# A layer's branches with finer points, twelve gate groups of the first merge made earlier, and a reordered start

## The reference

```
xn = RMSNorm(x);  z = xn @ w_in              # queries, keys, values, pool input, gates ...
ya = sliding-window attention (128) with sinks and a relative-position bias
yb = trailing means of windows 2/4/8/16 minus the token, @ w_pool
yc = mLSTM, chunks of 128, running-max stabiliser, gated and normed
merged = sum over a, b, c of sigmoid(g_b) * (y_b @ w_br_b)    # g_b: 1024 columns of z each
x = x + merged @ w_out
q = RMSNorm(x) @ wq;  top 16 x top 16 keys for 8 heads -> 16 experts a head, 128 a token
x = x + sum over 128 experts of gate * gelu(x . u[e]) * v[e]
```

## Time and profile before

| | us |
|---|---|
| median of three runs | 3836.78 |
| the execution profiled | 3825.35 |
| its span, first to last instruction | 3823.5 |
| TensorE busy | 3160.3 (83%) |
| VectorE busy | 2255.4 (59%) |
| ScalarE busy | 1102.1 (29%) |
| GpSimd busy | 1172.0 (31%) |
| read from and written to HBM | 344 GB/s over the span |
| mean granted clock of TensorE | 0.931 of 2.4 GHz |

### The profile page before, as it was taken

The page is one execution under the profiler, slowest core; times in us unless marked ns, Lnnn a source line. Parts: engine busy times, 40 slices in busy tenths (PEclk is TensorE's granted clock), DMA queues, the critical chain, the costliest instruction groups (busy, mean ns, idle before and its releaser), DMA issues. The chain is left out here.

```text
span 3823.5 us, 31573 instructions
## 1 busy us (share of the span) xinstructions
PE 3160.3 (83%) x10006; PEld 1820.0 (48%) x10006; DVE 2255.4 (59%) x5201; ACT 1102.1 (29%) x3314; POOL 1172.0 (31%) x1038
## 2 busy tenths in 40 slices
PE   7798879979989799769979799762699898777777
PEld 4487634546655444436656444431366563222222
DVE  1411777774657767664657688661555487775444
ACT  1210233432223324332223323340221233332222
POOL 0000333333333243333324233230233234443443
PEclk9899989989999899889999899885899999999999
DMA  5134899879999999779999899873899799999998
GB/s 168 60 124 159 348 365 383 349 297 396 420 394 403 365 403 412 303 303 404 420 384 407 349 403 398 324 266 139 331 375 392 278 399 397 421 421 422 421 420 358
DMA packets 204913, 1317.39 MB, mean 345 GB/s; under 512 B 23235, under 2 KB 27387, under 8 KB 72098
## 3 DMA queue, kind: packets, MB, share of 16 engines
q0 software_dynamic: 148608, 1082.20, 69.9%
q1 hardware_dynamic: 52681, 220.59, 15.4%
q10 hardware_dynamic: 3456, 12.58, 0.8%
HBM read 1298.97 MB, written 17.64 MB: 344 GB/s over the span
## 5 line engine op out<-in xcount | busy, mean ns | idle before, releaser
L1857 POOL DMA_INDIRECT arena<-uv,eidx x1032 | 1171.4, 1135 | 2623.2 <-PE ps L889 1889.5
L889 PE MATMUL ps<-arena,dgs 128*128 128x512 f32 x3412 | 1631.1, 622 | 268.4 <-ACT dgs L1189 244.4
L1428 DVE CUSTOM_DVE_ANT_0 arena<-arena,xx 128x1024 f32<-128x1024 f32 x1024 | 1231.8, 1220 | 583.9 <-DMA arena<-uv,eidx 559.5
L889 PEld LDWEIGHTS ps<-arena,dgs 128*128 128x128 f32 x3412 | 652.3, 198 | 1083.1 <-issue 675.0
L1170 ACT ACTIVATE gel<-dots 128x2 f32<-128x2 f32 x516 | 104.4, 202 | 1585.3 <-DVE dots L1428 1584.4
L922 PE MATMUL ps<-wbuf,xT 128*128 128x420 f32 (+1 forms) x1152 | 428.5, 522 | 7.7 <-DMA wbuf<-w_z 6.6
L1069 PE MATMUL ps<-xT,wbuf 128*128 128x256 f32 (+1 forms) x1536 | 356.8, 386 | 5.2 <-DMA wbuf<-w_merge 3.0
L1069 PEld LDWEIGHTS ps<-xT,wbuf 128*128 128x128 f32 x1536 | 295.1, 193 | 74.2 <-issue 19.4
L922 PEld LDWEIGHTS ps<-wbuf,xT 128*128 128x128 f32 (+1 forms) x1152 | 205.2, 181 | 231.1 <-issue 221.7
L1189 ACT ACTIVATE dgs<-cst,wgt 128x128 f32<-128x128 f32 x853 | 305.3, 395 | 16.7
L1662 DVE SCALAR_TENSOR_TENSOR T<-T,ps 128x256 f32<-128x256 f32 (+1 forms) x96 | 40.6, 423 | 434.5 <-PE ps L1073 434.5
(11 more groups left out here) (352 smaller groups left out, 1901.5 us busy)
## 6 DMA issues: line engine op xcount, KB each, us to landing
wbuf<-w_merge SPq DMA_DIRECT2D x96, 768.0 KB, 8.4
wbuf<-w_z SPq DMA_DIRECT2D x64, 840.0 KB, 8.6
wbuf<-w_q SPq DMA_DIRECT2D x64, 512.0 KB, 8.1
arena<-uv,eidx POOLq DMA_INDIRECT x1032, 11.4
wbuf<-w_o SPq DMA_DIRECT2D x32, 512.0 KB, 7.4
xin<-x_prompt SPq DMA_DIRECT2D x8, 1024.0 KB, 8.3
grow<-gains SPq DMA_DIRECT2D x8, 512.0 KB, 9.1
xin<-biasfull SPq DMA_DIRECT2D x4, 1024.0 KB, 4.9
```

What stands on the lines that cost most here:

```text
L889: done = mm(ps[:, half, :], dgs[:, j, :], ring[:, j, row_], start=(q == 0), stop=(q == P - 1), skip_group_check=True)
L1428: v.tensor_tensor_reduce(ring[:, j, 0:D], ring[:, j, 0:D], x, 1.0, 0.0, ALU.mult, ALU.add, dots[:, j:j + 1]).then_inc(s["dotted"], 1)
L1857: g.indirect_dma_start(ring[:, j, :], None, uv, bass.IndirectOffsetOnAxis(ap=experts, axis=0)).then_inc(got[j], 16)
```

## The change

- *Finer points.* `BRANCH` has 10 points of equal weight instead of 7; a stretch keeps its number of slots. Pass 1: 2, 2, 2, 2, 2, 0, 2, 2, 2, 2 slots a tile instead of 4, 2, 2, 2, 2, 2, 4; tile 0 of pass 2: 2, 2, 4, 2, 2, 2, 2, 2, 2, 4 instead of 4, 4, 2, 2, 4, 2, 6. The new TensorE places are behind S, behind the first scores (ahead of the 8-column broadcast), behind the inter-chunk product, behind the second scores, and on so to the end; ScalarE has its points 0 to 2 behind its three copies.
- *Order in a tile.* The cumulative sum (4 columns) is made first, into bank 3; the pool's means go to bank 7; VectorE copies the mLSTM's q behind the diagonal instead of ahead of it, and the second half of P ahead of the h chain.
- *Early gates.* In pass 0 the gates of the first 12 merge units are made in the branches, 6 a tile (1, 2, 1, 1, 1 behind points 2, 4, 6, 8, 9), into banks 0 and 1; ScalarE copies each to `early`, in the idle gather ring, and makes the tanh from there in the merge. Their weights come in two parts: the gates' two thirds behind the projection's weights, the branch third in the merge.
- *Start.* The tables but `cst` are issued behind the first two weights, the bucket matmul stands behind the projection's unit 0, `spread_bias` behind it as before, and the norm doesn't wait for them.
- *Tile by tile.* The projection's first unit waits for the xT of its tile only.

```diff
-BRANCH = (4, 4, 2, 2, 4, 2, 6)
+BRANCH = (2.4,) * 10
+EARLY = 12
+EARLY_AT = {2: 1, 4: 2, 6: 1, 8: 1, 9: 1}
...
             sp.dma_start(xin[:, :, :], x_prompt[0:NT].rearrange("t p d -> p t d")).then_inc(s["x_in"], 16)
-            sp.dma_start(cst[:, :], consts[:, 0:C_KEEP]).then_inc(s["setup"], 16)
...
+            sp.dma_start(cst[:, :], consts[:, 0:C_KEEP]).then_inc(s["consts_in"], 16)
+            def load_tables():
+                sp.wait_ge(s["init_v"], 1)
+                sp.dma_start(T[0:32, 512:520], rel).then_inc(s["setup"], 16)
+                sp.dma_start(T[:, 0:512], consts[:, C_KEEP:C_ALL]).then_inc(s["setup"], 16)
...
-                weights(w_z, ..., [lambda: load_bias(p)] if p else [spread_bias], ...)
+                weights(w_z, ..., [lambda: load_bias(p)] if p else [load_tables, spread_bias], ...)
+                if p == 0:
+                    weights(w_merge, (12, P), EARLY, s["gate_mm"], 0, 1, part=lambda i: (0, 2 / 3))
...
                 weights(w_merge, (12, P), 3 * KC, s["br_mm"], 3 * KC * p, 1, ...,
+                        part=lambda i: (2 / 3 if p == 0 and i < EARLY else 0, 1))
...
             def project(p):
...
                     for i, (t, rows_) in enumerate(tiles):
+                        if c == 0:
+                            pe.wait_ge(s["xT_ready"], norms(p, 0, i + 1))
...
+                    if p == c == 0:
+                        buckets()
+            def gates_early(units):
+                for u in range(gates_done[0], gates_done[0] + units):
+                    pe.wait_ge(w_in[u % 2], 16 * ((NZ + u) // 2 + 1))
+                    if u >= 2:
+                        pe.wait_ge(s["early_out"], u - 1)
+                    wv = wbuf[:, u % 2, 0:KC * P].rearrange("p (c n) -> p c n", c=KC)
+                    for c in range(KC):
+                        last = mm(ps[:, u % 2, 0:TOK], wv[:, c, :], xT[:, c, 0:TOK], start=(c == 0), stop=(c == KC - 1))
+                    last.then_inc(s["gate_mm"], 1)
...
                     scores(0).then_inc(s["scores_a"], 1)
+                    point(p, "b", t, 2)
+                    if p == 0:
+                        gates_early(EARLY_AT[2])
                     pe.wait_ge(s["M_ready"], here)
+                    pe.wait_ge(s["pooled_ready"], here)
                     mm(ps[:, 7, 0:8], last_row, bM, start=True, stop=True).then_inc(s["bcast_mm"], 1)
-                    point(p, "b", t, 1)
...
+                    point(p, "b", t, 3)
                     pe.wait_ge(s["tile_v"], tile.at("La_ready", NT * p + t + 1))
                     scores(1).then_inc(s["scores_mm"], 1)
-                    point(p, "b", t, 2)
+                    point(p, "b", t, 4)
+                    if p == 0:
+                        gates_early(EARLY_AT[4])
...
+                    if p or k >= EARLY:
+                        for c in range(KC):
+                            last = mm(ps[:, 2 + 2 * b, m], wv[:, c, :], xT[:, c, m], start=(c == 0), stop=(c == KC - 1))
+                        last.then_inc(s["gate_mm"], 1)
```

More of the change, by code:

```diff
@@ L366, in gated_after, with unit @@
             return PH * (g // NT) + q // PK + 1 if g < TILES else PH * PASSES + 1
+        def unit(p, i):
+            return p * UNITS + i + (EARLY if p or i >= NZ else 0)
         def norms(p, which, i):
@@ L765, in _, with weights @@
             used = [None]
-            def weights(src, shape, count, sem, base, per, between=(), later=None):
+            def weights(src, shape, count, sem, base, per, between=(), later=None, part=lambda i: (0, 1)):
                 width = int(np.prod(shape))
                 def load(i, k):
-                    sp.dma_start(wbuf[:, k, 0:width], src[i]).then_inc(w_in[k], 16)
+                    lo, hi = (int(width * x) for x in part(i))
+                    sp.dma_start(wbuf[:, k, lo:hi], src[i][:, lo:hi]).then_inc(w_in[k], 16)
                 for k in range(2):
@@ L978, in branches @@
                     last.then_inc(s["S_mm"], 1)
+                    point(p, "b", t, 1)
                     pe.wait_ge(s["qT_ready"], here)
                     pe.wait_ge(s["kT_ready"], here)
+                    pe.wait_ge(s["tile_v"], tile.at("b_ready", NT * p + t + 1))
                     def scores(kv):
@@ L1019, in branches @@
                     last.then_inc(s["state_mm"], 1)
-                    point(p, "b", t, 4)
+                    point(p, "b", t, 6)
+                    if p == 0:
+                        gates_early(EARLY_AT[6])
                     for half in range(2):
@@ L1039, in branches @@
                     last.then_inc(s["pooly_mm"], 1)
-                    point(p, "b", t, 6)
+                    point(p, "b", t, 9)
+                    if p == 0:
+                        gates_early(EARLY_AT[9])
                 done = NT * (p + 1)
@@ L1067, in merge @@
                     wv = wbuf[:, k % 2, 0:12 * P].rearrange("p (c n) -> p c n", c=12)
-                    for c in range(KC):
-                        last = mm(ps[:, 2 + 2 * b, m], wv[:, c, :], xT[:, c, m], start=(c == 0), stop=(c == KC - 1))
-                    last.then_inc(s["gate_mm"], 1)
+                    if p or k >= EARLY:
+                        for c in range(KC):
+                            last = mm(ps[:, 2 + 2 * b, m], wv[:, c, :], xT[:, c, m], start=(c == 0), stop=(c == KC - 1))
+                        last.then_inc(s["gate_mm"], 1)
                     point(p, "m", k, 0)
@@ L1245, in project, with gates_early @@
                         f(z[:, :, CO0:CO0 + 512], z[:, :, CO0:CO0 + 512], ACT.Sigmoid).then_inc(s["co_sig"], 1)
+            gates_kept = [0]
+            def gates_early(units):
+                for u in range(gates_kept[0], gates_kept[0] + units):
+                    act.wait_ge(s["gate_mm"], u + 1)
+                    f(early[:, u, :], ps[:, u % 2, 0:TOK], ACT.Copy).then_inc(s["early_out"], 1)
+                gates_kept[0] += units
             def branches(p):
@@ L1281, in branches @@
                     last.then_inc(s["P_exp"], 1)
-                    point(p, "b", t, 4)
+                    point(p, "b", t, 5)
+                    point(p, "b", t, 6)
+                    if p == 0:
+                        gates_early(EARLY_AT[6])
                     act.wait_ge(s["PTa_tr"], here)
@@ L1616, in branches @@
                     last.then_inc(s["CT_ready"], 1)
-                    point(p, "b", t, 5)
+                    point(p, "b", t, 7)
+                    dve.wait_ge(s["PT_tr"], here)
+                    dve.wait_ge(s["PV_mm"], before)
+                    v.tensor_copy(R[:, 3072:4096], psf[:, 1024:2048]).then_inc(s["PTd_ready"], 1)
+                    point(p, "b", t, 8)
                     dve.wait_ge(s["tile_v"], tile.at("h_ready", NT * p + t + 1))
```

127 lines of the change are left out of this document (74 added, 53 removed).

## The result

The changed kernel takes 3749.36 us (median of 4 runs, 3747.1 to 3755.32) against 3834.9 for the kernel before on the same chip (3830.9 to 3838.83): ratio 0.978, 95% interval 0.976 to 0.980. The profiled execution has a span of 3745.3 us against 3823.5, so 78.2 us less.

What follows compares the result with a forecast made beforehand. Bounds were seen by stage: tail by DMA, first merge by TensorE, branches of passes 1 to 3 by nothing for long, with gathers starving. Terms 11 + 22.4 - 32 - 3 - 30 = -31.6 from 3836.8 gave 3805, stated as 3806; range 3778 to 3836.

Steps and rivals of the forecast that it cites:

- the whole is wrong if the branches of pass 2 fall below 135: Sign against the whole forecast: branches of pass 2 falling below 135 us, or still taking over 155.
- Part 1: Start: first projection begins 5.0 us earlier, but its third weight lands at 50.9 behind the bias write; cost +11 us.
- the weight passes the bias write: Rival, chance 0.08: the third projection weight isn't held by the bias write; the start brings -5, total 3789 us.
- Part 2: Twelve gate groups moved from the first merge into pass 0's branches: branches +22.4 us, merge -32, together -9.6.
- what each delays: First tile of pass 0: gate groups followed on the earlier timeline; 20.8 us of matmuls cost 11.2 a tile.
- More work should hold it at 2.4 GHz more often: Pass 0's branches: added gate matmuls should keep TensorE's clock, 0.78 before, at the full rate more often.
- Part 3: Finer points in the branches of passes 1 to 3: -3, -15 and -15 us; bounds +10 to -62 together.
- -7.5 a tile, -15 in pass 2: Branches of pass 2: tile 0 falls from 75.7 to 68 us with 6 of waits left; doubled for two tiles.
- the "62" without waits: Tile 0 of pass 2: length in us from following three queues with gathered data always there.
- the ring runs free: Rival, chance 0.17: gather starvation goes wholly, four tiles of passes 2 and 3 fall to 62; branches -62, total 3776 us.
- TensorE's queue: Rival, chance 0.12: it becomes the bound in branches of passes 1 to 3, 8 us more a tile, total 3853.
- The points don't do what they say: Rival, chance 0.10: VectorE's waits only move, gathers' round trip being the limit; branches -8 in all, total 3830 us.

Runs made afterwards that it cites:

- Experiment 6: The changed kernel with tables, bucket matmul and bias write put back ahead of the first projection as in the kernel before: 3736.44 us.
- 5: The changed kernel with the bias table written from ScalarE's queue in two steps, through a 16 KB DRAM copy, outermost dimension 16 instead of 8: 3734.34 us.
- experiment 4: The changed kernel with the bias table's write issued from ScalarE's queue instead of SyncE's: 3741.53 us.
- experiment 3: The changed kernel with the old order within a branch tile; points, early gates and start stay as changed: 3755.03 us.
- Experiment 1: The changed kernel with the branches' slots spread as coarsely as before (4,4,0,2,2,4,0,2,0,6) over its ten places: 3812.11 us.
- 7: The changed kernel with the coarse spread (4,4,0,2,2,4,0,2,0,6) in the branches of the last pass alone: 3778.55 us.
- experiment 9: The changed kernel with the coarse spread in the last pass's branches and the sample stage's 127-partition K and V loads cut in two: 3728.24 us.

## Why the prediction was wrong

All three parts had the sign that was forecast; the sum was 47 us too small on the profiled execution (-31.6 against -78.2), and the time fell below the range. Three terms failed: the cost of the gates in the branches of pass 0 (11 us too high, because the tile's own matmuls were taken at their old lengths), the gain of the finer points (18 too small), and the stages behind the branches, put at nothing (18). The rest, 1.6 of gain in the start and 2.5 of loss in the first merge, is small. The time also moved past one of the prediction's own signs, that the whole is wrong if the branches of pass 2 fall below 135: they took 134.0.

**Part 1, right.** +9.4 for +11, with the third weight awaited until 49.15 (50.9 forecast) and 20.73 us idle (21). Experiment 6 gives the loss back, 5 shows that the write's form is the cause. The rival "the weight passes the bias write" is dead, and experiment 4 adds that a queue of its own doesn't free the weight either.

**Part 2, the merge right, the branches twice too dear.** The first 12 merge units took 254.2 - 222.1 = 32.1, so 2.7 each for 2.5, and the merge's term came out at -29.5 for -32. The branches grew by 11.3 for 22.4. The forecast of 22.4 was for gates and order together, with 1.2 + 0.2 a tile for the order already taken off. The step that failed is the timeline "what each delays": it put each group, at the full clock, between matmuls that kept the lengths of the earlier trace rows. Up to the start of the softmax this held in the first tile: 22.1 us from the tile's start, 22.7 forecast. Behind it, the two products L1010 and L1017 took 3.6 from start to end before and 1.9 now (L1051, L1058), and the two halves of PV with the pool's product 5.4 before and 2.9 now. So PV came 35.0 in for 38.6, and the next tile 41.5 in for 47.3. In the first tile, before and then after:

```profile
141.06 2.09 PE L1010 MATMUL ps<-arena,grow 128*128 128x129 f32 x8 [5.52 <-DVE grow L1580]
142.95 1.93 PE L1017 MATMUL ps<-arena,T 128*128 128x129 f32 x8
...
155.66 1.76 PE L1038 MATMUL ps<-T,wpool 128*128 128x128 f32 x8
```

```profile
155.69 1.06 PE L1058 MATMUL ps<-arena,T 128*128 128x129 f32 x8
...
168.55 1.16 PE L1084 MATMUL ps<-T,wpool 128*128 128x128 f32 x8
```

"More work should hold it at 2.4 GHz more often" was right but stood in the text without a price, and the bounds looked at the clock on the costly side only ("the groups at 1.2 GHz half of the time"). The granted clock rose from 0.78 to 0.99.

The order was priced right for the first tile with gates, 1.4 us (experiment 3), and too low for the rest: 8.5 in the second tile, most of it clock, and 3.4 and 6.9 without gates. The kernel without gates shows where it helps by itself, in its first tile (start 132.9):

```profile
139.87 0.39 PE L1029 MATMUL ps<-T,cst 128*128 128x8 f32 x2
...
153.53 1.04 PE L1066 MATMUL ps<-cst,R 128*128 128x128 f32 x8
...
159.62 1.98 PE L1078 MATMUL ps<-R,vprev 128*64 128x512 f32 x4 [1.32 <-DVE R L1696]
...
165.57 0.63 PE L977 MATMUL ps<-cst,arena 128*128 128x128 f32 x4
```

Counted from the tile's start, the 8-column matmul comes 7.0 in and PV 26.7; in the earlier trace rows (start 122.2) they come 8.5 and 29.8 in. So 1.5 are won at first and 1.6 more up to PV. The first was forecast at 1.2, the second at 0.2.

**Part 3, the mechanism right in part, the size wrong.** 18 of the 47 us are here: -33 was forecast for the branches of passes 1 to 3, -51.1 measured. First, "-7.5 a tile, -15 in pass 2" took the gain of tile 0 for both. The second tile was 84.7 long and had 20.9 us of waits for gathers, more than tile 0's 17.8; it fell to 70.6, by 14.1. Second, tile 0 itself fell by 12.4, not 7.5: to 63.4, not 68. The waits for gathers left in it are 7.2 us (6 forecast), so it was the "62" without waits that was some 6 too high: apart from these waits the tile took VectorE's busy time of 56.0 and hardly more. VectorE waited 0.4 for TensorE, where the hand-followed queues had 3.2 for the 8-column matmul alone. Whether a tile can come down to 56 isn't shown; the shortest of pass 2 in any run took 61.7 (experiment 3). Windows of tiles 0 and 1 of pass 2 in the kernel after:

```profile
1522.70:1586.10 63.40, 52.65 (x191) 28.63 (x189) 56.01 (x101) 27.88 (x82) 27.09 (x23) 0.92 1.00 404
1586.10:1656.70 70.60, 57.62 (x199) 31.97 (x198) 56.29 (x101) 31.11 (x86) 29.35 (x24) 0.91 0.94 381
```

404 GB/s at a DMA share of 1.00: in tile 0 the transfers are at their bound. (The stage came to a share of 0.97 where 0.87 was forecast.) For this tile the rival "the ring runs free" had the better number (62), and my objection to it (11.4 us landing of eight buffers) weighed little: 7.2 us. The other three tiles, the second ones with the stage's end, took 70.6, 69.3 and 67.9, nearer to the 68 that was forecast. Third, the forecast put the whole gain down to the spread. Experiment 1 gives it 34.5 of the 51.1; 16.6 are there with the old bursts at the new places, and the prediction had no term for them.

**The sum had no term for what follows.** The sample stage (-11.5) and the merge of pass 2 (-5.6) were put at nothing, since no point of theirs changed; with 1.2 us of other stages they are 18 more of the 47. Experiments 1, 7 and 9 show that the spread in the branches ahead of it is worth 12 us to the sample stage; experiment 1 that the merge's 5.4 go with the spread too. How the one stage hands it to the next is read from the issues of gathers (experiment 9), not tried alone.

**The rivals.** TensorE's queue did not become the bound: the wait for the 8-column matmul that I gave 3.2 us in every tile is 4.1 a tile in pass 0, 3 in pass 1, and 1.0 in both tiles of pass 2 together. Its condition was a clock below 0.75, and the clock rose instead, to 0.88 to 0.92. "The points don't do what they say" is refuted by experiment 1, -63.

**The range.** The miss of part 3 alone would have stayed in it (3806 - 18 = 3788). What took the time out of it are the branches of pass 0, which grew by 11.3 with +17 as their lowest bound, and the stages behind the branches, which had no bounds; the medians also differ by 7 us more than the profiled executions. And its lower edge, 3778, lies above the 3776 of the rival "the ring runs free", which the text counts among those that it takes in.

## What to carry to other kernels

Spread the freeing of buffers evenly along the instruction streams that share them (here points of 2 to 4 slots instead of up to 6; finer or coarser steps weren't tried), and look at how a stage ends as something handed to the next one: it was worth 12 us there. When work goes into the gaps of a TensorE at a low granted clock, price what its own matmuls get back, not only what the added ones delay. When a stage's waits are to go, read them tile by tile and not one tile for all. And look at the outermost dimension of each slow transfer first: here the change moved a write that ran at 52 GB/s into a worse place, while its shape, and that of two loads at 20 GB/s, was worth 62 us more than the change gave.

## What the runs showed of the hardware that was not expected

- Loads of 127 rows ran at 20 GB/s and held the issuing queue for 43.2 and 29.4 us; cutting them into 112 and 15 rows took 48 us off the kernel.
- A transfer in SyncE's queue took 18 us to land beside a write from 8 partitions that ScalarE's queue had issued, against 4.3 us usually.
- Adding 21.8 us of matmuls to each of two tiles in which TensorE had gaps raised the granted clock of the stage from 0.82 to 0.99; the first tile grew by 8.8 us (32.7 to 41.5), the second, with the stage's end, by 12.8 (36.2 to 49.0).
- With the old order, the second of these tiles had 10 us at a granted clock of 0.50 (180 to 190 us), and a group of 16 matmuls took 6.37 us in it, 3.72 otherwise.
- The spread of the points changes nothing in what is computed or moved, and was worth 63 us (1.7%).
